# Modulation panels computed in pairs, each 32-column group of TensorE with an output column tile of its own

## The chip, the cores and the metric

One core of a Trainium2 chip (trn2) runs the whole step. The metric is the device time of one execution in microseconds (us); lower is better. Three runs of the kernel before gave 1291.79, 1292.11 and 1295.12 us, median 1292.11.

## The reference, cut to what matters

One layer of a hybrid decoder, for 256 prompt tokens and 8 sequences of 8 sampled tokens (320 tokens, width 1024, all float32). Nine modulation vectors of width 1024 come from the 9 conditioning rows c (one of the prompt, eight of the samples), and shift, scale and gate every branch:

```python
mod = jax.nn.silu(c) @ p['ada_w'] + p['ada_b']          # (9, 1024) @ (1024, 9216)
sh1, sc1, g1, sh2, sc2, g2, sh3, sc3, g3 = jnp.split(mod, 9, axis=-1)
u = rmsnorm(x, norm_ff1) * (1 + sc1) + sh1
x = x + 0.5 * g1 * swiglu(u, ff1_w1, ff1_w3, ff1_w2)    # "up1" (w1, w3) and "down1" (w2)
...                                                     # norm_mix with sh2, sc2; mixer; g2
...                                                     # norm_ff2 with sh3, sc3; "up2", "down2"; g3
```

## The kernel before, in words

**Layout.** Activations stand transposed: features on the 128 partitions, the 320 tokens along the free dimension. Every dense product goes by units of 128 output columns: eight or more blocks of 128 rows of the weights, each an instruction of 128x320 (`mm`, L908). Float32 is split in two parts (`w_hi` + `w_lo`, `u_hi` + `u_lo`), so a unit has three passes of 8 instructions: high by high, low by high, high by low. ScalarE (ACT) makes `w_hi` of a unit two units ahead (`high_ahead`, L1679 to L1690), VectorE (DVE) makes `w_lo` (`low_ahead`, L2304 to L2315).

**The stream.** `unit_order` (L162) writes out the order of all units, and `Stream` gives each a panel in a ring of four 1 MB slots and a PSUM bank. SyncE (SP) loads the panels in that order (`load`, L581); it waits until the unit that last read the slot is done. TensorE (PE) executes its program in order.

**The modulation.** `ada_w` has 36 panels of 1024 x 256 ("ada" units). `ada` (L961) takes the activations as the stationary operand: `c_t` holds silu(c) transposed, 9 columns for each block of 128 rows; the instruction reads 32 columns of it. The array is used as four column groups of 32: block kc goes to group kc % 4 and writes PSUM partitions 32g to 32g+31 with all 256 columns of the panel. So each group holds the sum over two of the eight row blocks, and the four groups must still be added. ACT copies the bank to `mod_row` (`ada_row`, L1692). `mod_columns` (L1046) transposes it by two PE transposes of 128x128 into `aux`. `mod_add` on DVE (L2317) reduces over the four groups (L2321), then adds the bias (L2322).

Panels 0 to 3 hold sh1, 4 to 7 hold sc1, each panel 256 of the 1024 features. These eight are ahead of "up1", in the order `ADA_HEAD` = 4, 0, 5, 1, 6, 2, 7, 3. The other 28 follow later two at a time, behind units of up1 (18 panels, L37), down1 (6, L38) and up2 (4, L39). There the transposes of two panels are issued just ahead of the next two panels (`panel`, L1126).

**The front.** The order of each engine is written out by hand. PE (L1078 to L1103): transposes of c; panel 4; transposes of the packed parameters; then the panels one by one, each followed by `mod_columns` of the one before; x is turned (`turn_x`, three transposes for each of 8 blocks) in two halves, behind the second and the third panel; the sum of squares behind the fourth. ACT (L1782 to L1801): `ada_row` of each panel, squares and copies of x in two halves, the table load for the square root (`load_root`), `root`, `first_norm_high` of the four pairs of feature blocks (L1716), with `w_hi` of up1's first unit ahead of the fourth. DVE (L2416 to L2433):

```python
            for i in range(4):
                mod_add(st.at["ada", ADA_HEAD[i]])
            dve.wait_ge(S["x_read"], KD)
            inverse_root(0)
            mod_add(st.at["ada", ADA_HEAD[4]])
            first_norm(0)
            mod_add(st.at["ada", ADA_HEAD[5]])
            first_norm(1)
            first_norm(2)
            mod_add(st.at["ada", ADA_HEAD[6]])
            first_norm_low(0)
            mod_add(st.at["ada", ADA_HEAD[7]])
            first_norm(3)
            first_norm_low(1)
```

`first_norm(pair)` (L2404) makes the gain (L2409) and two tiles x * gain / rms (L2337). ACT adds the shift (L1714), POOL does the same for the sampled tokens (L706, L707) and ACT copies those (L1675). `first_norm_low` (L2412; L2352, L2345) makes the low parts. Up1's first two units run in one piece (`dense_two`, L910).

Of the kernel before, what the change touches and what calls it, by code (L numbers as in the profile page):

```python
# [7 lines left out]
ALU = mybir.AluOpType  # L8
# [27 lines left out]
ADA_HEAD = (4, 0, 5, 1, 6, 2, 7, 3)  # L36
# [22 lines left out]
def ada_place(p):  # L59

    return ADA_HEAD.index(p) if p < len(ADA_HEAD) else p

# [21 lines left out]
class Stream:  # L84
# [12 lines left out]
    def __init__(self, order):  # L97
# [4 lines left out]
        for name, q in order:  # L102
# [99 lines left out]
def build(nc, io, out):  # L202
# [5 lines left out]
    with ctx:  # L208
# [444 lines left out]
        def _(pool):  # L653
# [41 lines left out]
            def first_samples():  # L695
# [65 lines left out]
            def row_fills():  # L761

                pool.wait_ge(S["gates_mm"], 1)
                pool.wait_ge(S["mod_turned"], ADA_LAST_DOWN + 1)
# [137 lines left out]
        def _(pe):  # L902
# [58 lines left out]
            def ada(u):  # L961
                w = panel_dst(u)
                pe.wait_ge(slot_in[u.slot], u.arrivals)
                if u.uses:
                    pe.wait_ge(bank_free[u.bank], u.uses)
                for kc in range(KD):
                    g = kc % 4
                    ins = mm(banks[u.bank][32 * g:32 * g + 32, 0:256], c_t[:, NSEQ * kc:NSEQ * kc + 32], w[:, kc, :], kc < 4, kc >= 4)
                ins.then_inc(unit_done, 1)

            def shift_rows(n, shift, u):

                pe.wait_ge(slot_in[u.slot], u.arrivals)
                pe.wait_ge(S["mod_read"], 4 * shift + 8)
# [71 lines left out]
            def mod_columns(u):  # L1046
# [38 lines left out]

            for i, a in enumerate(ADA_HEAD):
                u = st.at["ada", a]
                ada(u)
                if a == ADA_HEAD[0]:
# [4 lines left out]
                if i > 0:  # L1094
                    mod_columns(st.at["ada", ADA_HEAD[i - 1]])
                if i == 1 or i == 2:
                    for kc in range(4 * (i - 1), 4 * i):
                        turn_x(kc)
                if i == 3:
# [3 lines left out]
            mod_columns(st.at["ada", ADA_HEAD[-1]])  # L1103
# [22 lines left out]
            def panel(u, pending):  # L1126

                if u.q % 2 == 0:
                    for v in pending:
                        mod_columns(v)  # L1130
                    pending = []
                ada(u)
                return pending + [u]
# [47 lines left out]
            for u in st.of("qk"):  # L1181
# [9 lines left out]
                if u.q == 4:  # L1191
                    pe.wait_ge(S["gate_lin"], 1)
                    pe.wait_ge(S["mod_read"], ADA_LAST_DOWN + 1)
# [477 lines left out]
        def _(act):  # L1671
# [20 lines left out]
            def ada_row(u):  # L1692
                p = ada_place(u.q)
                act.wait_ge(unit_done, u.done)
                if p >= 2:
                    act.wait_ge(S["mod_turned"], p - 1)
                copy(mod_row[p % 2][:, :], banks[u.bank][:, 0:256]).then_inc(bank_free[u.bank], 1)
# [18 lines left out]
            def first_norm_high(pair):  # L1716
                for kc in range(2 * pair, 2 * pair + 2):
# [64 lines left out]
            for i, a in enumerate(ADA_HEAD):  # L1782
                u = st.at["ada", a]
                ada_row(u)
# [3 lines left out]
                if i == 1 or i == 2:  # L1788
                    for kc in range(4 * (i - 1), 4 * i):
                        act.wait_ge(S["x_turned"], kc + 1)  # L1790
                        nc.scalar.activation(sq[:, kc, :], aux[kc % 2][:, 0:T], ACT.Square).then_inc(S["sq_ready"], 1)
                        copy(x_t[:, kc, :], aux[kc % 2][:, 0:T]).then_inc(S["x_read"], 1)
                if i == 2:
                    load_root()
                if i == 3:
                    root(0)
                if i >= 5:
                    first_norm_high(i - 5)
# [491 lines left out]
        def _(dve):  # L2290
# [820 lines left out]
```

## Time and profile before

| what | value |
|---|---|
| time, median of three runs | 1292.11 us |
| span of the profiled execution | 1291.4 us |
| PE busy | 1256.7 us, 97% of the span |
| DVE busy | 782.7 us, 61% |
| ACT busy | 624.3 us, 48% |
| DMA over the span | 241.57 MB, 187 GB/s |

The span is all that the profile gives of the profiled execution's own time; it lies 0.7 us below the median of the three runs. In the profile, PE is TensorE's matmul side and PEld its weight loads. "PEclk" and the last columns of the windows give the clock that TensorE was granted, as a part of full speed. In rows of the timeline the first number is the start, the second the length of the stretch from the first start to the last end, and xN the number of instructions. A float32 matmul or transpose of the `ada` kind is two instructions in the trace for one in the code (a panel is x16 for eight calls); a transpose is one.

### The profile page before, as it was taken

To read this page: it belongs to the slowest core of one execution; us is meant where nothing else is said; L and a number is where in the kernel's file an instruction comes from. 1 tells how busy PE (TensorE), PEld (TensorE's weight loads), DVE (VectorE), ACT (ScalarE), POOL (GpSimd) and SP (SyncE) were. 2 spreads that over 40 slices of the span, in tenths; PEclk is the share of its full clock that TensorE was granted. 3 is DMA by queue.
4 is the path that set the end of the run, shared out by engine and by line. 5 is a ranking of instruction groups with operands and counts; after the bars stand their busy time and mean duration, and the time that the engine had idled before them with its cause. 6 is when DMAs were issued, how large, how long until landed. Compare 5 with 4: busy or idle time off the path is not lost.

```text
span 1291.4 us, 22833 instructions
## 1 busy us (share of the span) xinstructions
PE 1256.7 (97%) x9132; PEld 1152.1 (89%) x9132; DVE 782.7 (61%) x1368; ACT 624.3 (48%) x1101; POOL 222.3 (17%) x393
## 2 busy tenths in 40 slices
PE   6899999999999899999999999999999999999997
PEld 3699999999997777779999889888999989999997
DVE  0734444545896456856379877865576884554433
ACT  3433333434757646655356675554652453333432
POOL 4100000011551222211023333322500310000000
PEclk9899999999999999999999999999999999999998
DMA  9976777776333689886664375464436446554541
GB/s 281 247 242 212 244 252 231 215 221 208 99 99 112 219 281 334 297 278 191 188 196 143 111 212 167 136 205 149 132 108 186 133 129 208 184 164 131 152 141 41
DMA packets 258863, 241.57 MB, mean 187 GB/s; under 512 B 8607, under 2 KB 242479, under 8 KB 258710
## 3 DMA queue, kind: packets, MB, share of 16 engines
q1 hardware_dynamic: 249262, 211.03, 53.7%
q0 software_dynamic: 9024, 28.91, 6.7%
q8 instruction: 73, 1.20, 0.4%
q10 hardware_dynamic: 472, 0.17, 0.1%
q14 instruction: 32, 0.26, 0.1%
HBM read 209.88 MB, written 30.21 MB: 186 GB/s over the span
## 4 chain that ended last, share of the span: by engine, by line
PE 61%; DVE 5%; ACT 2%; issue 1%; POOL 0%; ACTq 0%; DVEq 0%; POOLq 0%
PE bank L908 52%; PE aux L908 6%; PE aux L905 2%; DVE w_lo L2313 1%; DVE arena L2526 1%; PE bank L905 1%; ACT w_hi L1689 1%; DVE arena L2524 0%; ACT arena L1675 0%; DVE stats L2758 0%; ACT vp L1675 0%; DVE arena L2530 0%; ACT u_hi L1714 0%; POOL arena L751 0%; DVE arena L2337 0%
## 5 line engine op out<-in xcount | busy, mean ns | idle before, releaser
L2313 DVE TENSOR_TENSOR w_lo<-ring,w_hi 128x1024 fp32r<-128x1024 f32 (+1 forms) x264 | 336.8, 1276 | 374.9 <-ACT w_hi L1689 370.4
L1689 ACT ACTIVATE w_hi<-ring 128x1024 fp32r<-128x1024 f32 (+1 forms) x264 | 289.7, 1097 | 505.4 <-PE bank L908 486.3
L908 PE MATMUL bank<-u_hi,w_hi 128*128 128x320 f32 x1504 | 264.0, 317 | 4.1 <-issue 1.5
L908 PE MATMUL bank<-u_hi,w_lo 128*128 128x320 f32 x1504 | 251.3, 309 | 0.4 <-DVE w_lo L2313 0.4
L908 PE MATMUL bank<-u_lo,w_hi 128*128 128x320 f32 x1504 | 250.6, 309 | 0.0
L908 PEld LDWEIGHTS bank<-u_hi,w_hi 128*128 128x128 f32 x1504 | 228.8, 189 | 20.9 <-issue 14.0
L908 PEld LDWEIGHTS bank<-u_hi,w_lo 128*128 128x128 f32 x1504 | 228.1, 188 | 0.9 <-DVE w_lo L2313 0.9
L908 PEld LDWEIGHTS bank<-u_lo,w_hi 128*128 128x128 f32 x1504 | 228.2, 188 | 0.0
L905 PE MATMUL aux<-ident,arena 128*128 128x128 f32 (+5 forms) x408 | 61.7, 282 | 14.8 <-ACT arena L1778 8.7
L905 PEld LDWEIGHTS aux<-ident,arena 128*128 128x128 f32 (+5 forms) x408 | 45.5, 145 | 27.3 <-issue 16.5
L713 POOL TENSOR_TENSOR arena<-x_t,gain 128x64 f32<-128x64 f32 x16 | 4.8, 299 | 354.8 <-DVE x_t L2385 354.8
L908 PE MATMUL bank<-ff_hi,w_hi 128*128 128x320 f32 x352 | 57.8, 311 | 0.0
L908 PE MATMUL bank<-ff_hi,w_lo 128*128 128x320 f32 x352 | 56.8, 308 | 0.0
L908 PE MATMUL bank<-ff_lo,w_hi 128*128 128x320 f32 x352 | 56.8, 308 | 0.0
L908 PEld LDWEIGHTS bank<-ff_hi,w_hi 128*128 128x128 f32 x352 | 52.6, 188 | 1.6 <-issue 1.6
L908 PEld LDWEIGHTS bank<-ff_hi,w_lo 128*128 128x128 f32 x352 | 52.9, 187 | 0.0
L908 PEld LDWEIGHTS bank<-ff_lo,w_hi 128*128 128x128 f32 x352 | 52.9, 187 | 0.0
L1675 ACT ACTIVATE arena<-bank 128x256 f32<-128x256 f32 (+4 forms) x134 | 43.3, 355 | 17.5 <-PE bank L908 14.5
L691 POOL TENSOR_TENSOR arena<-arena 128x320 f32<-128x320 f32 x12 | 10.4, 869 | 239.9 <-ACT arena L1701 226.5
L908 PE MATMUL bank<-arena 32*128 32x128 f32 (+6 forms) x496 | 51.0, 355 | 0.4 <-DVE arena L2920 0.4
L2526 DVE SCALAR_TENSOR_TENSOR arena<-arena,par 128x344 f32<-128x344 f32 x80 | 46.7, 583 | 3.9 <-POOL arena L751 1.8
L908 PE MATMUL bank<-y_hi,w_hi 128*128 128x320 f32 x272 | 45.8, 309 | 0.0
(390 smaller groups left out, 1617.2 us busy)
## 6 DMA issues: line engine op xcount, KB each, us to landing
ring<-in_w_in SPq DMA_DIRECT2D x52, 1024.0 KB, 5.6
ring<-in_ff_w SPq DMA_DIRECT2D x44, 1024.0 KB, 5.5
ring<-in_ada_w SPq DMA_DIRECT2D x36, 1024.0 KB, 7.3
ring<-in_ff_w SPq DMA_DIRECT2D x32, 704.0 KB, 4.7
arena<-in_state_mlstm_C SPq DMA_DIRECT2D x22, 512.0 KB, 6.3
out_s_C<-arena POOLq DMA_DIRECT2D x22, 512.0 KB, 5.8
ring<-in_w_pa SPq DMA_DIRECT2D x8, 1024.0 KB, 6.6
arena<-in_state_ssm SPq DMA_DIRECT2D x32, 256.0 KB, 4.6
```

The lines of the kernel that those rows point to most:

```text
L691: ins = nc.gpsimd.tensor_tensor(sq[:, 0, :], sq[:, 0, :], sq[:, kc, :], ALU.add)
L713: nc.gpsimd.tensor_tensor(sequences(xg_s[n][:, kc, :]), sequences(x_t[:, kc, TP:T]), gain[:, kc, 1:NSEQ].unsqueeze(2).to_broadcast([128, S ...
L905: return nc.tensor.transpose(dst, src, ident[0:rows, 0:rows])
L908: return nc.tensor.matmul(dst, lhs, rhs, start=first, stop=last)
L1675: return nc.scalar.activation(dst, src, ACT.Copy, scale=scale)
L1689: nc.scalar.activation(w_hi[v.split_no % 2][:, 0:v.kc, :], panel_part(v), ACT.Copy).then_inc(S["hi_done"], 1)
L2313: V.tensor_tensor(w_lo[r][:, 0:v.kc, :], panel_part(v), w_hi[r][:, 0:v.kc, :].bitcast(FP32), ALU.subtract)\
L2526: ch.link(V.scalar_tensor_tensor(out=a, in0=p[:, tap:tap + CONVW], scalar=par[:, c + w_col + tap * tiles:c + w_col + tap * tiles + 1], in1 ...
```

## The change

- The panels are computed two at a time (`ada_pair`). Column groups 0 and 1 take the two 128-column halves of the first panel, groups 2 and 3 those of the second. Every group runs over all eight row blocks, so nothing is left to be added up over groups. A pair writes 128 columns of one bank instead of 256 columns of two.
- ACT copies 128 columns once for a pair, PE transposes once instead of four times, and DVE does one addition of the bias straight out of PSUM (128 x 36) instead of two reductions and two additions. `mod_read` and `mod_turned` now count pairs.
- `ADA_HEAD` becomes 4, 5, 0, 1, 6, 7, 2, 3: scale of the first half, shift of the first half, scale and shift of the second half.
- The front is rewritten for pairs: x is turned whole behind the first pair; ACT and DVE have new orders; `first_norm_high`, `first_norm_low` and POOL's part now wait for the pair that holds their shift.

```diff
-ADA_HEAD = (4, 0, 5, 1, 6, 2, 7, 3)
+ADA_HEAD = (4, 5, 0, 1, 6, 7, 2, 3)
...
 def ada_place(p):
-    return ADA_HEAD.index(p) if p < len(ADA_HEAD) else p
+    return (ADA_HEAD.index(p) if p < len(ADA_HEAD) else p) // 2
...
+            if second_of_pair(name, q):          # name == "ada" and q % 2 == 1
+                u.opens = False
+                bank_at[name, u.own] = bank_at[name, u.own - 1]
...
@@ POOL, first_samples @@
                     pool.wait_ge(S["xr_ready"], 2 * pair + 1)
+                    pool.wait_ge(S["mod_read"], panels_read(pair) + 1)
...
@@ PE @@
-            def ada(u):
-                w = panel_dst(u)
-                pe.wait_ge(slot_in[u.slot], u.arrivals)
-                if u.uses:
-                    pe.wait_ge(bank_free[u.bank], u.uses)
-                for kc in range(KD):
-                    g = kc % 4
-                    ins = mm(banks[u.bank][32 * g:32 * g + 32, 0:256], c_t[:, NSEQ * kc:NSEQ * kc + 32], w[:, kc, :], kc < 4, kc >= 4)
-                ins.then_inc(unit_done, 1)
+            def ada_pair(first, second):
+                for u in (first, second):
+                    pe.wait_ge(slot_in[u.slot], u.arrivals)
+                if second.uses:
+                    pe.wait_ge(bank_free[second.bank], second.uses)
+                for kc in range(KD):
+                    for g in range(4):
+                        u = (first, second)[g // 2]
+                        ins = mm(banks[u.bank][32 * g:32 * g + 32, 0:128], c_t[:, NSEQ * kc:NSEQ * kc + 32],
+                                 panel_dst(u)[:, kc, g % 2 * 128:(g % 2 + 1) * 128], kc == 0, kc == KD - 1)
+                        if kc == KD - 1 and g % 2:
+                            ins.then_inc(unit_done, 1)
...
@@ mod_columns @@
-                for j in range(2):
-                    ins = turn(aux[2 + r][:, j * 128:(j + 1) * 128], mod_row[r][:, j * 128:(j + 1) * 128], 128)
-                ins.then_inc(S["mod_turned"], 1)
+                turn(aux[2 + r][:, 0:128], mod_row[r][:, 0:128], 128).then_inc(S["mod_turned"], 1)
...
@@ PE, the front @@
+            for i, (first, second) in enumerate(head):
+                ada_pair(first, second)
+                if i == 0:
...                                              (transposes of the parameters, as before)
+                    for kc in range(2):
                         turn_x(kc)
+                    mod_columns(second)
+                    for kc in range(2, KD):
+                        turn_x(kc)
+                if i == 1:
+                    mod_columns(second)
                     pe.wait_ge(S["x_read"], KD)
                     sum_squares_most(0)
                     sum_squares_last(0)
+                if i >= 2:
+                    mod_columns(second)
...
@@ ACT, the front @@
+            for i in range(4):
+                ada_row(st.at["ada", ADA_HEAD[2 * i + 1]])
                 if i == 0:
...                                              (par, as before)
+                    for kc in range(KD):
...                                              (square and copy of x, as before)
+                    load_root()
+                if i == 1:
+                    root(0)
                 if i == 2:
+                    first_norm_high(0)
+                    first_norm_high(1)
+            first_norm_high(2)
             high_ahead(st.at["ada", ADA_HEAD[-1]], st.at["up1", 0])
             first_norm_high(3)
...
@@ DVE, mod_add @@
-                m = mod[:, 2 * p:2 * p + 2, :]
-                ch.link(V.tensor_reduce(m, aux[2 + r][:, 0:256].rearrange("p (j g s) -> p j s g", j=2, g=4)[:, :, 0:NSEQ, :], AX.X, ALU.add))
-                V.tensor_tensor(m, m, par[:, 2 * p:2 * p + 2].unsqueeze(2).to_broadcast([128, 2, NSEQ]), ALU.add).then_inc(S["mod_read"], 1)
+                V.tensor_tensor(mod[:, 2 * p - 2:2 * p + 2, :], aux[2 + r][:, 0:128].rearrange("p (g s) -> p g s", g=4)[:, :, 0:NSEQ],
+                                par[:, 2 * p - 2:2 * p + 2].unsqueeze(2).to_broadcast([128, 4, NSEQ]), ALU.add).then_inc(S["mod_read"], 1)
...
@@ DVE, the front @@
+            mod_add(st.at["ada", 5])
             dve.wait_ge(S["x_read"], KD)
             inverse_root(0)
             first_norm(0)
             first_norm(1)
+            mod_add(st.at["ada", 1])
+            first_norm_low(0)
+            mod_add(st.at["ada", 7])
             first_norm(2)
             first_norm(3)
             first_norm_low(1)
+            mod_add(st.at["ada", 3])
             first_norm_low(2)
             low_ahead(st.at["ada", ADA_HEAD[-1]], st.at["up1", 0])
             first_norm_low(3)
```

## Rows read from the trace of the kernel before

**Rows 1.** The page: busy time, share of the span, instructions.
```profile
PE 1256.7 (97%) x9132; PEld 1152.1 (89%) x9132; DVE 782.7 (61%) x1368; ACT 624.3 (48%) x1101; POOL 222.3 (17%) x393
```

**Rows 2.** Windows: length, busy (x) of PE, PEld, DVE, ACT, POOL, clock, DMA, GB/s.
```profile
53.20:320.00 266.80, 266.79 (x2075) 252.00 (x2076) 131.46 (x225) 98.31 (x141) 9.42 (x16) 1.00 0.75 228
```

**Rows 3.** Timeline, a late pair of panels between two units of up1.
```profile
86.13 0.60 PE L905 MATMUL aux<-ident,arena 128*128 128x128 f32 x4
...
86.66 1.45 PEld L908 LDWEIGHTS bank<-ring,c_t 128*32 128x32 f32 x32 [0.17 <-issue]
86.66 1.93 PE L908 MATMUL bank<-ring,c_t 128*32 128x256 f32 x32
```

**Rows 4.** The tile c_t: all weight loads of the panels, min/median/max ns.
```profile
L908 PEld LDWEIGHTS bank<-ring,c_t x576: 106/110/178, 10.0 to 1122.5; 128*32 128x32 f32 x192
```

**Rows 5.** Timeline, narrow windows (86.9 and 87.05 on) of that pair.
```profile
86.90 0.13 PEld L908 LDWEIGHTS bank<-ring,c_t 128*32 128x32 f32 x4
...
86.66 0.64 PE L908 MATMUL bank<-ring,c_t 128*32 128x256 f32 x8
...
86.66 0.85 PE L908 MATMUL bank<-ring,c_t 128*32 128x256 f32 x12
```

**Rows 6.** Timeline: a copy to w_hi that waited for its DMA, and the unit that uses it.
```profile
165.01 1.06 ACT L1689 ACTIVATE w_hi<-ring 128x1024 fp32r<-128x1024 f32 x1 [3.18 <-DMA ring<-in_ff_w]
...
169.95 1.29 PE L908 MATMUL bank<-u_hi,w_hi 128*128 128x320 f32 x7
```

**Rows 7.** Timeline of the front: PE and what it feeds, to the reciprocal.
```profile
14.84 0.45 ACT L1675 ACTIVATE par<-aux 128x336 f32<-128x336 f32 x1 [2.34 <-PE aux L905]
...
16.43 1.93 PE L908 MATMUL bank<-ring,c_t 128*32 128x256 f32 x16 [1.63 <-DMA ring<-in_ada_w]
...
19.74 0.44 ACT L1791 ACTIVATE arena<-aux 128x320 f32<-128x320 f32 x1 [0.93 <-PE aux L905]
...
20.66 0.44 ACT L1791 ACTIVATE arena<-aux 128x320 f32<-128x320 f32 x1
...
30.70 1.30 PE L908 MATMUL aux<-arena,ones 128*128 128x320 f32 x4
...
31.93 1.07 PE L908 MATMUL bank<-ring,c_t 128*32 128x256 f32 x16
32.03 0.53 ACT L1709 ACTIVATE rs<-aux,eps_col 128x320 f32<-128x320 f32 x1 [1.02 <-PE aux L908]
...
33.77 2.14 DVE L2331 RECIPROCAL rs<-rs 128x320 f32<-128x320 f32 x1
```

**Rows 8.** Timeline of the front, from the gains to up1's first units.
```profile
38.53 0.17 DVE L2409 SCALAR_TENSOR_TENSOR gain<-mod,par 128x18 f32<-128x18 f32 x1
...
38.74 0.95 DVE L2337 SCALAR_TENSOR_TENSOR arena<-x_t,gain,rs 128x256 f32<-128x256 f32 x2
...
39.53 0.90 ACT L1714 ACTIVATE u_hi<-arena,mod 128x256 fp32r<-128x256 f32 x2
...
40.48 0.31 ACT L1675 ACTIVATE u_hi<-arena 128x128 fp32r<-128x128 f32 x1
...
41.39 0.28 DVE L2352 TENSOR_TENSOR u_lo<-arena,u_hi 128x128 fp32r<-128x128 f32 x1
41.60 1.03 DVE L2345 SCALAR_TENSOR_TENSOR u_lo<-arena,mod,u_hi 128x256 fp32r<-128x256 f32 x2
...
42.19 1.04 ACT L1689 ACTIVATE w_hi<-ring 128x1024 fp32r<-128x1024 f32 x1
...
53.21 1.40 PE L908 MATMUL bank<-u_hi,w_hi 128*128 128x320 f32 x8
```

**Rows 9.** Windows of the front (columns as rows 2).
```profile
18.30:24.20 5.90, 5.90 (x34) 2.87 (x30) 0.41 (x2) 3.45 (x9) 2.59 (x3) 1.00 1.09 348
...
43.30:50.00 6.70, 6.58 (x29) 5.85 (x30) 6.50 (x13) 2.16 (x4) 0.99 (x2) 0.66 1.02 203
```

**Rows 10.** DMA issues of the panel asked for at 30.3 us.
```profile
ring<-in_ada_w SPq DMA_DIRECT2D x1, 1024.0 KB, 5.1
```

More of the change, by code:

```diff
@@ L59, in ada_place, with panels_read, second_of_pair @@
 def ada_place(p):
-    return ADA_HEAD.index(p) if p < len(ADA_HEAD) else p
+    return (ADA_HEAD.index(p) if p < len(ADA_HEAD) else p) // 2
+def panels_read(end):
+    return ada_place(end)
+def second_of_pair(name, q):
+    return name == "ada" and q % 2 == 1
 def high_at(norm, kc):
@@ L1084, in _ @@
             pe.wait_ge(S["small_made"], 2)
[L1086 to L1089, printed above, removed]
+            head = [(st.at["ada", ADA_HEAD[i]], st.at["ada", ADA_HEAD[i + 1]]) for i in range(0, len(ADA_HEAD), 2)]
+            for i, (first, second) in enumerate(head):
+                ada_pair(first, second)
+                if i == 0:
                     pe.wait_ge(S["packs_in"], 11 * 16)
@@ L1093, in _ @@
                     turn(aux[0][:, 216:336], pk[0:120, 2, :], 120).then_inc(S["front_turned"], 1)
[L1094 to L1097, printed above, removed]
+                    for kc in range(2):
                         turn_x(kc)
-                if i == 3:
+                    mod_columns(second)
[3 more added lines that the diff above has]
+                    mod_columns(second)
                     pe.wait_ge(S["x_read"], KD)
@@ L1130, in panel @@
                         mod_columns(v)
-                    pending = []
-                ada(u)
-                return pending + [u]
+                    return []
+                ada_pair(st.at["ada", u.q - 1], u)
+                return [u]
             for u in st.range(("up1", 0), ("up1", 2 * KF - 1)):
@@ L1693, in ada_row @@
                 p = ada_place(u.q)
+                if not second_of_pair(u.name, u.q):
+                    return
                 act.wait_ge(unit_done, u.done)
@@ L1696, in ada_row @@
                     act.wait_ge(S["mod_turned"], p - 1)
-                copy(mod_row[p % 2][:, :], banks[u.bank][:, 0:256]).then_inc(bank_free[u.bank], 1)
+                copy(mod_row[p % 2][:, 0:128], banks[u.bank][:, 0:128]).then_inc(bank_free[u.bank], 1)
             def square(n, kc):
@@ L1716, in first_norm_high @@
             def first_norm_high(pair):
+                act.wait_ge(S["mod_read"], panels_read(pair) + 1)
                 for kc in range(2 * pair, 2 * pair + 2):
@@ L1787, in _ @@
                     copy(par[:, :], aux[0][:, 0:336]).then_inc(S["front_read"], 1)
-                if i == 1 or i == 2:
-                    for kc in range(4 * (i - 1), 4 * i):
+                    for kc in range(KD):
                         act.wait_ge(S["x_turned"], kc + 1)
@@ L2406, in first_norm @@
                 k = slice(2 * pair, 2 * pair + 2)
-                dve.wait_ge(S["mod_read"], 2 * pair + 2)
+                dve.wait_ge(S["mod_read"], panels_read(4 + pair) + 1)
                 g = par[:, 72 + 2 * pair:74 + 2 * pair].unsqueeze(2).to_broadcast([128, 2, NSEQ])
@@ L2412, in first_norm_low @@
             def first_norm_low(pair):
+                dve.wait_ge(S["mod_read"], panels_read(pair) + 1)
                 samples_low(0, 2 * pair, 2 * pair + 2)
                 tiles_low(0, 0, 2 * pair, 2 * pair + 2)
-            for i in range(4):
-                mod_add(st.at["ada", ADA_HEAD[i]])
+            mod_add(st.at["ada", 5])
             dve.wait_ge(S["x_read"], KD)
             inverse_root(0)
-            mod_add(st.at["ada", ADA_HEAD[4]])
             first_norm(0)
-            mod_add(st.at["ada", ADA_HEAD[5]])
             first_norm(1)
+            mod_add(st.at["ada", 1])
+            first_norm_low(0)
+            mod_add(st.at["ada", 7])
             first_norm(2)
-            mod_add(st.at["ada", ADA_HEAD[6]])
-            first_norm_low(0)
-            mod_add(st.at["ada", ADA_HEAD[7]])
             first_norm(3)
             first_norm_low(1)
+            mod_add(st.at["ada", 3])
             first_norm_low(2)
@@ L2441, in panel @@
                         mod_add(v)
-                    pending = []
-                return pending + [u]
+                    return []
+                return [u]
             for u in st.range(("up1", 0), ("up1", 2 * KF - 1)):
```

19 lines of the change are left out of this document (5 added, 14 removed).

## The prediction

> **What bounds the kernel now.** I read the page first: PE is busy for 1256.7 of 1291.4 us [rows 1]. Then windows: from the third unit of up1 to the start of the mixer PE is busy for 266.79 of 266.80 us [rows 2]. So behind the front a microsecond of work taken from PE is a microsecond gained, and work taken from ACT or DVE is worth nothing. The front (0 to 53.21 us) is another matter: there PE waits, and the path changes hands. The timeline shows it: PE with the panels and x until 31.9 us, root and reciprocal until 35.91 us [rows 7], then DVE, ACT and POOL by turns make u until ACT copies the first `w_hi` at 42.19 us, and the third unit of up1 starts at 53.21 us [rows 8]. Both places have to be costed, and they have different signs.
>
> **Part 1: the 14 pairs behind the front.** There are 576 matmuls of this kind, 32 for a pair, so 18 pairs [rows 4]; four lie in the front, 14 behind it. Before, a pair is 32 matmuls in eight sets of four that run side by side. The sets are 0.85 - 0.64 = 0.21 us apart [rows 5], and the pair takes 1.93 us with the end of the last one [rows 3]. After, there are 64 matmuls in sixteen sets, each over half the columns: 0.107 us a set if the columns set the pace, so 1.93 us again. The unknown is the weight loads, 64 for a pair in place of 32. Below: the loads of a set lie beside the matmuls of the set before, as now (32 loads keep PEld busy for 1.45 us inside the 1.93 us [rows 3]), and cost nothing; they can't gain anything, since the columns are the same. Above: the four loads of a set take 0.13 us [rows 5], and a set cannot be shorter than that: 16 x 0.13 = 2.08 against 1.71 us, 0.37 us a pair. I take nothing, because the recorded load (110 ns [rows 4]) is longer than a load keeps its successor waiting: these 128x128 transposes also need loads, and four of them with theirs went by in 0.60 us with the last one's end.
>
> PE's transposes fall from four to one for a pair. Four start 0.53 us before the panels' first matmul [rows 3]; that is 0.13 us each with the change to column groups, which stays. Without it I take half the pitch of a 256-column set, 0.11 us: 3 x 0.11 = 0.33 us a pair, 4.6 us for 14 pairs (5.6 us by 0.13).
>
> ACT's one copy for two and DVE's one addition for four instructions are hidden by PE and earn nothing. The first panel's slot comes free only at the end of the pair, 0.9 us later; SP's queue behind it (the next panels) starts later by that. What covers it: where ACT already waits for a DMA, the copy at 165.01 us, done at 166.07, is used at 169.95 [rows 6], 3.9 us of cover; seven copies wait so, and none of them has less than 3 us. If the cover were gone, it would cost up to 0.9 us for each of nine pairs in up1.
>
> Here a rule of the Trainium skill speaks against the change. In the trace, loads ran beside matmuls of all four column groups [rows 3, 5]. The page "TensorE: Matmul & The Clock Gate" (Part 3: Packing small matmuls) says that a load overlaps with matmuls in flight only when the row group differs; here every group uses all rows. By that rule twice the loads would stand open, which is the third rival below; the trace does not agree with it.
>
> **Part 2: the front up to the reciprocal.** The first pair needs the panel that PE waited for until 16.43 us [rows 7]; that stays. At half clock a panel took 1.93 us at 16.43 and 1.07 us at 31.93 [rows 7], which is TensorE's lower level (1.2 GHz) and its upper one (2.4 GHz); PE had then been busy without a break since 16.43. First pair: 3.7 us, to 20.1. Then three transposes of the parameters (some 0.8 us), ACT's copy of them (0.45 us), on which x now waits, and 0.93 us until ACT has the first block of x [rows 7]: 22.3 us. Blocks follow every 0.92 us (19.74, 20.66 [rows 7]), with one transpose between: the last is turned at 29.0 us. Second pair: half clock until about 31, as before, then full: 31.9 us (30.8 if the clock is up from the start, 32.7 if not at all). ACT's copy and one transpose, 0.6; sum of squares 1.30; root 0.53; reciprocal 2.14 [rows 7]: it ends at 36.5 us, against 33.77 + 2.14 = 35.9. Call this end R; 0.6 us later, between 0.5 us earlier and 1.4 later.
>
> **Part 3: the front from R on.** Now the hand-written order of DVE decides. Steps [rows 8]: the gain and two tiles 1.16 us (38.53 to 39.69); two tiles by ACT and the samples' copy behind POOL 1.3 us (39.53 to 40.79); low parts of a pair 1.24 us (41.39 to 42.63); `mod_add` now one instruction, 0.2 us. The sum: two gains with tiles 2.3; `mod_add` of the second pair, which ACT's first high part now needs, 0.2; ACT 1.3; low(0) 1.25; `mod_add` 0.2; two more gains with tiles 2.3; low(1) 1.25; only then `mod_add` of the last pair, which holds the shift of blocks 4 to 7, 0.25; ACT's high(2) 1.3: R + 10.35. ACT has `w_hi` of up1 behind that, 1.04, and PE starts at R + 11.5 = 48.0 us. Before, it started at 43.3, R + 7.4, as the shift was there before and only the tiles were waited for. So 4.7 us later: 4.1 from the order, 0.6 from R. From there to the third unit it was 9.9 us; at mean clock 0.66 in 43.3 to 50 [rows 9], so half clock for 4.6 us. PE had nearly stood still from 37 us on. It stands still for longer now, so I keep the half-clock stretch; but blocks 6 and 7 are less behind: 9.4 us. The front's end is then 4.7 - 0.5 = 4.2 us later. Nothing absorbs it: PE has no idle time afterwards.
>
> Cover in the front: the last two panels are asked for when the second pair is done, 31.9 us, since it holds slots 2 and 3. One asked for with an empty queue landed after 5.1 us [rows 10], the next follows 3.0 us behind (1.05 MB at 348 GB/s [rows 9]): 40.0 us. Half clock 3.7, copy and transpose 0.6: 44.3 us, and DVE asks for it at R + 8.85 = 45.3. Covered by 1.0 us. Up1's first panel lands 3 us behind, at 43, needed at 46.9. POOL's waits for the shifts lie inside the 1.3 us.
>
> **The sum.** +4.2 - 4.6 = -0.4. The profiled span of 1291.4 is 0.7 us below the median; against the median 1292.1 it gives 1291.7 us. About 0.3%, 3.9 us, is what a measurement of this kernel can tell from no change, so this is no change: a gain in the middle given away in the front.
>
> **Rivals.**
> 1. *The front costs almost nothing: faster.* The clock rises during the first pair, a denser stretch than any before, and is still up when up1 starts: R is 1.1 us earlier, the 4.6 us at half clock give back up to 2.3, of which I count 1.8, and the transposes are worth 0.13 each (1.0 more). 1291.7 - 3.9 = 1287.8 us. For it: 3.7 us of panels without a break. Against: PE stands for some 4 us before up1, and it came down before with less. Chance 0.14.
> 2. *The loads set the pace: slower.* In `ada_pair`, the four loads of a set take 0.13 us, the columns 0.107. It decides from the point where a set lasts over 0.13 us: 0.37 us a pair, 5.2 us for 14, which eats the transposes: 1296.9 us. For it: twice the loads with half the work over each. Against: they start together and lie over each other. Chance 0.17.
> 3. *The loads are not hidden at all,* the rule above: 16 x 0.13 = 2.1 us a pair on top, 29 us for 14, 1321 us. Against it stand the rows of before. Chance 0.02.
> 4. *The transposes were not on the path,* because what ends last is ACT's or DVE's copy of the weights: then only the front's 4.2 us stand, 1296.3 us. Against: PE never waited [rows 2]. Chance 0.05.
>
> The forecast has 0.62; its own range is 1289 to 1295.5 us (R from -1.1 to +0.8 about my value, loads up to 0.1 us a pair, transposes 0.11 to 0.13). Faster by over 0.3% is rival 1: 0.14. Slower is rivals 2 to 4: 0.24. Within: 0.62. The range that holds it 8 times in 10 reaches to rivals 1 and 2: 1288.0 to 1297.0.
>
> **What the profile after would show.** Part 1: 64 matmuls of 128x128 in about 1.9 us for a pair, one transpose ahead; over 2.2 us means rival 2. Part 2: reciprocal ends near 36.5. Part 3: first `w_hi` copy near 47 us in place of 42.2, with DVE the engine that ACT waited for; third unit near 57.4. I am wrong if up1 starts before 45 us, if a pair gets shorter than 1.8 us, or if PE waits for a panel in up1.

## The result and the profile after

The change made the kernel a little slower: 1296.49 us (1294.19 to 1297.53, 20 runs) against 1293.34 us (1289.78 to 1296.94, 20 runs) for the kernel before on the same chip. The ratio is 1.0019, interval 1.0012 to 1.0025, so +2.5 us of the kernel before. The forecast was 1291.7 us, 0.4 us below the median shown (1292.11). Set on that median the measured ratio is 1294.6 us: within the 0.3% of "no change" and inside the range of 1289 to 1295.5. But the kernel moved the other way than forecast, and its interval excludes no change. The raw median of 1296.49 us lies above that range and inside the wider one (1288.0 to 1297.0). The profiled execution has a span of 1295.1 us and a time of its own of 1296.83 us, 0.3 us above the median, so its rows can be read as those of a typical run.

The page after: span, busy time, share, instructions.
```profile
span 1295.1 us, 23766 instructions
...
PE 1253.9 (97%) x9654; PEld 1165.7 (90%) x9654; DVE 771.9 (60%) x1314; ACT 616.5 (48%) x1083; POOL 222.2 (17%) x393
```
Against [rows 1], PE is busy for 2.8 us less, and the span is 3.7 us longer. So the time is not in PE's work; it lies where PE waits.

**Behind the front.** Windows after (columns as in [rows 2]), from the third unit on:
```profile
57.10:320.00 262.90, 262.90 (x2421) 256.47 (x2422) 123.71 (x189) 92.96 (x129) 9.22 (x16) 1.00 0.76 232
```
Timeline after, the late pair of [rows 3] (start, length, engine):
```profile
90.03 0.27 PE L919 MATMUL aux<-ident,arena 128*128 128x128 f32 x1
90.23 1.69 PEld L922 LDWEIGHTS bank<-ring,c_t 128*32 128x32 f32 x64 [0.21 <-issue]
90.23 1.96 PE L922 MATMUL bank<-ring,c_t 128*32 128x128 f32 x64
...
92.11 1.44 PE L922 MATMUL bank<-u_hi,w_hi 128*128 128x320 f32 x8
```
The tile c_t after, all its weight loads (min/median/max ns):
```profile
L922 PEld LDWEIGHTS bank<-ring,c_t x1152: 106/110/178, 15.4 to 1127.1; 128*32 128x32 f32 x192
```
PE has no gap again. One transpose stands for four, and 64 matmuls take 1.96 us where 32 took 1.93. The 64 loads keep PEld busy for 1.69 us inside them.

**The front**, timeline after, from the first pair to the third unit of up1 (start, length):
```profile
15.48 3.64 PE L922 MATMUL bank<-ring,c_t 128*32 128x128 f32 x64 [5.73 <-DMA ring<-in_ada_w]
...
20.50 7.59 PE L919 MATMUL aux<-ident,arena 128*128 128x128 f32 x25 [0.63 <-ACT par L1693]
...
28.03 3.46 PE L922 MATMUL bank<-ring,c_t 128*32 128x128 f32 x64
...
33.27 1.96 PE L922 MATMUL bank<-ring,c_t 128*32 128x128 f32 x64
...
34.00 2.15 DVE L2350 RECIPROCAL rs<-rs 128x320 f32<-128x320 f32 x1 [10.91 <-ACT rs L1729]
...
41.12 3.64 PE L922 MATMUL bank<-ring,c_t 128*32 128x128 f32 x64 [5.14 <-DMA ring<-in_ada_w]
...
45.17 0.33 PE L919 MATMUL aux<-ident,arena 128*128 128x128 f32 x1 [0.41 <-ACT arena L1693]
45.54 0.20 DVE L2340 TENSOR_TENSOR mod<-aux,par 128x36 f32<-128x36 f32 x1 [0.29 <-PE aux L919]
...
47.02 1.04 ACT L1707 ACTIVATE w_hi<-ring 128x1024 fp32r<-128x1024 f32 x1
...
48.16 4.12 PE L922 MATMUL bank<-u_hi,w_hi 128*128 128x320 f32 x16 [2.65 <-issue]
...
57.09 1.41 PE L922 MATMUL bank<-u_hi,w_hi 128*128 128x320 f32 x8
```
The reciprocal ends at 36.15 (forecast 36.5), the first `w_hi` copy starts at 47.02 (forecast 47), up1 at 48.16 (48.0), the third unit at 57.09 (57.4) where it was 53.21 [rows 8]. Against that one profile the front is 3.9 us later. That so many rows fall on their forecasts is in part luck, as the repeats will show.

**What the forecast had not looked at:** three windows in the middle, after (columns as in [rows 2]), show half clock (1.2 GHz) for 2.2 to 2.8 of their 4 us:
```profile
326.00:330.00 4.00, 4.00 (x22) 4.00 (x22) 4.00 (x9) 0.47 (x1) 0.00 (x0) 0.73 0.00 0
438.00:442.00 4.00, 4.00 (x16) 1.19 (x9) 1.35 (x2) 0.89 (x3) 0.00 (x0) 0.65 0.00 0
1053.00:1057.00 4.00, 4.00 (x22) 4.00 (x22) 4.00 (x9) 0.46 (x1) 0.00 (x0) 0.73 0.00 0
```
The profile of before has the full clock at the same three places of its program. So the two profiles differ by -4.3 us (fourteen pairs), +3.9 (front) and, as the experiments will show, about +4 (three stretches at half clock): together the 3.7 us between the spans. The question is which of these the runs have, and which only these two profiles.

### The profile page after: what moved, and what is told of

It is laid out like the page before. It is cut to its first block, busy times and chain, and to the rows that moved or that the text cites. A ratio compares the mean times of both kernels' runs of the same rounds, so it can differ in the third digit from the quotient of the medians.

```text
span 1295.1 us, 23766 instructions
## 1 busy us (share of the span) xinstructions
PE 1253.9 (97%) x9654; PEld 1165.7 (90%) x9654; DVE 771.9 (60%) x1314; ACT 616.5 (48%) x1083; POOL 222.2 (17%) x393
## 4 chain that ended last, share of the span: by engine, by line
PE 61%; DVE 5%; ACT 2%; issue 1%; POOL 0%; ACTq 0%; DVEq 0%; POOLq 0%
PE bank L922 52%; PE aux L922 6%; PE aux L919 2%; DVE w_lo L2333 1%; DVE arena L2544 1%; PE bank L919 1%; ACT w_hi L1707 1%; DVE arena L2542 0%; ACT arena L1693 0%; DVE stats L2776 0%; DVE arena L2548 0%; ACT vp L1693 0%; ACT u_hi L1734 0%; POOL arena L765 0%; DVE arena L2356 0%
## 5 line engine op out<-in xcount | busy, mean ns | idle before, releaser
L922 PEld LDWEIGHTS bank<-u_hi,w_hi 128*128 128x128 f32 x1504 | 229.5, 190 | 18.3 <-issue 12.2
L919 PE MATMUL aux<-ident,arena 128*128 128x128 f32 (+4 forms) x354 | 54.2, 280 | 11.6 <-ACT arena L1799 8.8
L919 PEld LDWEIGHTS aux<-ident,arena 128*128 128x128 f32 (+4 forms) x354 | 38.9, 145 | 20.4 <-issue 14.1
L922 PE MATMUL bank<-ring,c_t 128*32 128x128 f32 x1152 | 40.1, 298 | 10.9 <-DMA ring<-in_ada_w 10.9
L922 PEld LDWEIGHTS bank<-ring,c_t 128*32 128x32 f32 x1152 | 34.7, 120 | 14.6 <-issue 14.2
```

The lines of the kernel that those rows point to most:

```text
L919: return nc.tensor.transpose(dst, src, ident[0:rows, 0:rows])
L922: return nc.tensor.matmul(dst, lhs, rhs, start=first, stop=last)
```

## The experiments

In all kernels "third unit" is the first matmul of up1's third unit, the first place with nothing to wait for; what comes behind it hardly differs wherever the middle is at full clock: span less third unit is 1238.1 to 1238.3 us in four profiles with the panels as before, and 1233.9 to 1234.4 us in five with the pairs.

**1. The two kernels again, and one half of the change at a time.** `before_again` is the kernel before, unchanged; `after_again` the changed one. In `rear_only` only panels 8 and later go by pairs:
```diff
+def second_of_pair(name, q):
+    return name == "ada" and q >= 8 and q % 2 == 1
...
-                ada(u)
-                return pending + [u]
+                    return []
+                ada_pair(st.at["ada", u.q - 1], u)
+                return [u]
```
`front_only` is the reverse: the eight panels of the front by pairs with the new front order, panels 8 and later as before.

> The kernel before once more, for a second profile. Theory A: its span may this time hold one or more stretches at half clock at the stalls near 322, 434 and 1046 us, each worth 1.1 to 1.7 us, and the profile of before was merely free of them. Theory B: none in the middle again. Ratio 1.000 in both.

> The changed kernel once more, for a second profile. Theory A (granted clock by luck): the stretches at half clock near 325, 437 and 1052 us of the first profile come from where the chip's grid of clock decisions happens to lie against three stalls that both kernels have; then this profile shows other ones, or none, the time stays about 2.4 to 3 us over the kernel before. Theory B (they belong to the change): the same three stretches again, at the same stalls.

> Pairs only for the 28 panels behind the front; the eight of the front and the whole front as before. By the sum of the prediction (transposes 0.33 us a pair, loads hidden): 4.4 us faster than before, ratio 0.9966. If weight loads or something else behind the front ate the gain: ratio 1.000 or above. If the half-clock stretches belong to the pairs behind the front: about 4 us of the gain is missing and the profile shows them.

> Pairs only for the eight panels of the front, with the new order of x, ACT and DVE; the 28 panels behind as before. By the sum of the prediction: third unit of up1 starts 3.9 to 4.2 us later and nothing gives it back: ratio 1.0032. If the front's loss is absorbed later: 1.000. If it also moves stalls so that half clock is granted more often: over 1.004.

| kernel | median us (lowest to highest, runs) | ratio to before, interval |
|---|---|---|
| before_again | 1294.74 (1291.06 to 1297.35, 12) | 1.0014, 1.0001 to 1.0027 |
| after_again | 1295.25 (1293.64 to 1297.71, 12) | 1.0020, 1.0007 to 1.0032 |
| rear_only | 1288.41 (1286.17 to 1293.73, 12) | 0.9973, 0.9958 to 0.9988 |
| front_only | 1300.27 (1299.78 to 1301.45, 6) | 1.0059, 1.0042 to 1.0076 |

The two halves have opposite signs, as forecast: the pairs behind the front gain, the front loses. `front_only` lost more than expected: 0.0059, where the sum gave 0.0032 and the interval starts at 0.0042. Its profile shows one part of it: behind the third unit it takes 1241.8 us instead of 1238.2, 3.6 us more, and two stretches at half clock near 438 and 1054 us make up about 3.1 of them. The two halves together (-3.5 and +7.6 us) give 4.1 us where the whole change gave 2.5; their intervals of about 2 us each leave open whether they simply add. The repeat of the unchanged kernel shows how little one ratio can carry here: 1.0014 with nothing changed. And its profile has a front of another length, in the same instructions. Timeline of `before_again`:
```profile
15.92 1.93 PE L908 MATMUL bank<-ring,c_t 128*32 128x256 f32 x16 [1.70 <-DMA ring<-in_ada_w]
21.88 1.93 PE L908 MATMUL bank<-ring,c_t 128*32 128x256 f32 x16
27.25 1.07 PE L908 MATMUL bank<-ring,c_t 128*32 128x256 f32 x16
...
31.74 2.15 DVE L2331 RECIPROCAL rs<-rs 128x320 f32<-128x320 f32 x1
...
40.17 1.04 ACT L1689 ACTIVATE w_hi<-ring 128x1024 fp32r<-128x1024 f32 x1
...
51.17 1.40 PE L908 MATMUL bank<-u_hi,w_hi 128*128 128x320 f32 x8
```
The fourth panel already goes at the full clock (1.07 us at 27.25); in the profile shown, PE was at half clock until about 31 us. The third unit is 2.0 us earlier. In `rear_only` the third panel was already fast, and the third unit stood at 50.61:
```profile
21.64 1.07 PE L921 MATMUL bank<-ring,c_t 128*32 128x256 f32 x16
```
The changed kernel's front varies as much. `after_again` has the same three stretches at half clock in the middle, but its third unit is 3.3 us earlier than in `after`:
```profile
19.14 2.77 PE L919 MATMUL aux<-ident,arena 128*128 128x128 f32 x13 [0.63 <-ACT par L1693]
...
30.86 2.15 DVE L2350 RECIPROCAL rs<-rs 128x320 f32<-128x320 f32 x1 [9.97 <-ACT rs L1729]
...
53.84 1.40 PE L922 MATMUL bank<-u_hi,w_hi 128*128 128x320 f32 x8
```
A warning on one column: for 18.3 to 24.2 us [rows 9] prints a clock of 1.00, though the panel in that stretch took 1.93 us, the time at half clock. In the front the panels' lengths are the better guide. Timeline of the kernel before:
```profile
22.39 1.93 PE L908 MATMUL bank<-ring,c_t 128*32 128x256 f32 x16
```

**2. The clock behind the front taken away.** The fill is work that changes no output: matmuls of 128 columns into columns of a bank that nobody reads, where PE waits behind the first gate of a branch and ahead of the state's tails.
```diff
+            def warm(dst, n):
+                for _ in range(n):
+                    mm(dst[:, 384:512], ident[:, :], ones[:, :])
...
                     for kc in range(KD):
+                        if i == 0:
+                            warm(aux[3], (2, 0, 1, 1, 3, 1, 1, 1)[kc])
                         pe.wait_ge(S["u_hi_ready"], high_at(n, kc))
...
+                if n == 1:
+                    pe.wait_ge(S["n_new"], 1)
+                    pe.wait_ge(S["den_read"], 1)
+                    warm(banks[2], 12)
```
(The eight numbers add up to 10 for each branch; the expectation of `after_warm` says 11.) The fill went into the kernel before, into `rear_only` and into the changed one. The fourth kernel, `front2`, is the changed one with another front order and no fill: the second pair stands between the two halves of x, both halves' sums are done ahead of the third pair, third and fourth pair go one behind the other with their transposes behind both, and DVE adds the columns of a pair as soon as they are there:
```diff
             mod_add(st.at["ada", 5])
+            mod_add(st.at["ada", 1])
             dve.wait_ge(S["x_read"], KD)
             inverse_root(0)
             first_norm(0)
             first_norm(1)
-            mod_add(st.at["ada", 1])
-            first_norm_low(0)
             mod_add(st.at["ada", 7])
+            mod_add(st.at["ada", 3])
             first_norm(2)
+            first_norm_low(0)
             first_norm(3)
             first_norm_low(1)
-            mod_add(st.at["ada", 3])
             first_norm_low(2)
```

> The same filling in the kernel before, which showed no half clock behind these stalls in two profiles. Theory clock: nothing to gain or at most 1 us (some of its runs have a lower mean clock), ratio 0.999 to 1.000. If filling shortens the kernel by 3 us here too, it is not what sets the two kernels apart.

> Pairs only behind the front, with the filling. Theory clock: the one stretch of half clock (429 us) is gone, and the whole 4.4 us of the transposes shows: ratio 0.9955 to 0.9965, against 0.9973 without the filling.

> The changed kernel with idle TensorE work (matmuls of constants into unused PSUM columns) put into the three stalls behind which half clock was granted: 11 ahead of up1's successors' normed units each time, 12 ahead of the second tails' transpose. Theory clock (the pairs move the stalls to where the clock falls, and that is the missing 3 to 4 us): no half clock at 321, 434 and 1048 us any more, 3.5 to 4 us faster than the changed kernel, ratio to before 0.999. Theory other (the half clock is an accident of the profiled runs and the loss lies elsewhere): ratio stays at 1.002 or rises with the extra work.

> The changed kernel with another order in the front alone: second pair between the two halves of x (so that its slots are free 5 us earlier), third and fourth pair next to each other, and DVE adds both ahead of the third gain. By the prediction's part 3, the order cost 4.1 us from the reciprocal on; this should give most of it back: up1 starts near 43.5 us in place of 48 (45 in the second profile), 4 us faster than the changed kernel, ratio near 0.999. If the front's loss came from the clock alone, no change: 1.002.

| kernel | median us (lowest to highest, runs) | ratio to before, interval |
|---|---|---|
| before_warm | 1290.60 (1288.46 to 1291.47, 9) | 0.9979, 0.9969 to 0.9989 |
| rear_warm | 1285.90 (1284.82 to 1288.25, 5) | 0.9946, 0.9934 to 0.9959 |
| after_warm | 1292.49 (1290.73 to 1293.47, 11) | 0.9996, 0.9984 to 1.0008 |
| front2 | 1294.03 (1292.15 to 1294.46, 11) | 1.0006, 0.9996 to 1.0017 |

Windows of `after_warm` at the same three places:
```profile
326.00:330.00 4.00, 4.00 (x30) 4.00 (x29) 4.00 (x10) 1.06 (x2) 0.00 (x0) 1.00 0.00 0
438.00:442.00 4.00, 4.00 (x27) 2.98 (x22) 2.99 (x3) 1.16 (x3) 0.77 (x1) 1.00 0.01 4
1053.00:1057.00 4.00, 4.00 (x30) 4.00 (x29) 3.93 (x10) 2.53 (x3) 0.00 (x0) 1.00 0.28 82
```
The first window holds 30 matmul instructions where the changed kernel had 22. Each stretch cost 1.16 to 1.64 us by the shift of what follows it. What PE did ahead of the first, in the changed kernel's timeline:
```profile
322.68 1.12 PE L922 MATMUL bank<-u_hi,w_hi 128*128 128x320 f32 x4 [0.60 <-ACT u_hi L1693]
...
324.38 1.84 PE L922 MATMUL bank<-u_hi,w_hi 128*128 128x320 f32 x4 [0.59 <-ACT u_hi L1734]
...
326.02 2.29 PE L922 MATMUL bank<-u_hi,w_lo 128*128 128x320 f32 x8
```
Two waits of 0.6 us for ACT, then a pass of eight matmuls in 2.29 us where it takes 1.33. The profile of before has the same two waits (0.58 and 0.59 us) and no half clock behind them, so the wait alone does not decide it. (Ahead of the second stretch stands one wait of 2.8 us, in both kernels.) All three stretches are in both profiles of the changed kernel and in that of `front2`, two in `front_only`, one in `rear_only`, none in two of before.

But my expectation that before gains at most 1 us by the fill fell: it gained 2.3 to 2.7 us, so many of its runs have such stretches too. The mean clocks of the timed runs bear this out. Of the 67 runs of before beside these kernels, 26 have 0.994, as the profile of `before_again`, with a median of 1291.30 us; the other 41 have 0.989 to 0.992, with a median of 1293.93. With the middle filled, all nine have 0.993 or 0.994. So both profiles of before are of the quicker kind, and `before_again`'s (1291.06 us) was the fastest of its twelve runs.

By the ratios the fill gains 3.0 us for the changed kernel and 2.7 us for before. The stretches explain what the two profiles differ by behind the front; of what the medians differ by they explain 0.3 us, give or take some 2 us by their intervals.

With the fill behind the front, the changed kernel is still 1.9 us slower than before (2.2 by the ratios), and 6.6 us slower than the pairs alone. That is most of the measured change, and it is in the front. `rear_warm` gained more than the 0.9955 to 0.9965 that I expected, since before itself gains by the fill.

`front2` shows which part of the front is the order of DVE and ACT. Its timeline:
```profile
34.05 2.15 DVE L2355 RECIPROCAL rs<-rs 128x320 f32<-128x320 f32 x1 [4.42 <-ACT rs L1734]
36.16 1.96 PE L922 MATMUL bank<-ring,c_t 128*32 128x128 f32 x64 [0.90 <-DMA ring<-in_ada_w]
...
42.09 1.04 ACT L1712 ACTIVATE w_hi<-ring 128x1024 fp32r<-128x1024 f32 x1
...
52.80 1.40 PE L922 MATMUL bank<-u_hi,w_hi 128*128 128x320 f32 x8
```
The first `w_hi` copy starts 5.9 us behind the reciprocal's end, where the changed kernel took 10.9 and the one before 6.3 (42.19 - 35.91). From the reciprocal's end to the third unit it takes 16.6 us, where before took 17.3 and the changed kernel 20.9: the order alone takes back all that Part 3 of the prediction counted as lost. But the reciprocal itself ends at 36.20, late as in the changed kernel. The third unit at 52.80 is 4.3 us earlier than in `after` and 1.0 us earlier than in `after_again`. The ratio with its unfilled middle is 1.0006, 1.7 us better than the changed kernel and not the 4 that I expected.

**3. The half clock in the front taken away too.** More fill of the same kind (`ident` by `ident`), in the waits of the front: in `before_hot` and `rear_hot` 6 ahead of the first panel, 6 around the parameters' transposes, 10 and 3 ahead of the last two panels' transposes, 5 behind them; in `after_hot`
```diff
+                if i == 0:
+                    hot(10, 3)
+                if i == 3:
+                    hot(20)
                 ada_pair(first, second)
...
                 if i >= 2:
                     mod_columns(second)
+                if i == 3:
+                    hot(18)
```
and in `front2_hot` 10, 6 and 14 at the same places.

> The kernel before with the fill of before_warm and, in the front too, 30 more matmuls of 128 columns whose result nobody reads, where TensorE waits for DMA or for ScalarE. My theory (the chip gives the front's first full clock at 19 to 31 us from one run to the next, and half clock once more behind the front's last waits; both are only luck of how busy TensorE was): the clock rises by 20 us in the profile, the 6.8 us at half clock near 37 to 41 us are gone or shorter, the reciprocal ends at 32 to 33 us, the third unit starts near 48.5 instead of 49.5, and the time is 1288.5 to 1290.5, 0.5 to 2 us under before_warm's 1290.6. Rival (the front is bound by DMA and by VectorE, its clock costs nothing): 1290.6, no change.

> Pairs only behind the front, with the fill of rear_warm and the same 30 matmuls in the front as in before_hot. Fourteen pairs are worth 0.31 us each plus the first-unit shifts, 4.3 to 4.7 us: so before_hot less 4.5, 1284.0 to 1286.0. Rival as for before_hot: 1285.9, as rear_warm.

> The change with the fill of after_warm and 48 such matmuls in the front: 10 ahead of the first pair, 20 ahead of the fourth pair while it waits for its DMA, 18 behind its transpose. My theory (the new front loses 4.5 us from the reciprocal on by VectorE's order and has nothing to do there with the clock; what it loses ahead of the reciprocal is mostly the clock): reciprocal end near 34, dense start near 46, third unit near 55, time 1289.5 to 1291.5, some 5 us over rear_hot and 0 to 1.5 over before_hot. Rival (the front's loss is the clock, which the filled front does not have): within 2 us of rear_hot, under 1288.

> The other front order (both halves of x around the second pair, column adds ahead of the reciprocal) with the fill behind the front and 30 such matmuls in the front. My theory: front2's reciprocal was late (36.2) for its clock and for the one long row of work ahead of it, and its order from there on costs only 7 us to the first copy of weights as before, so with a warm clock the third unit starts near 50.5 and the time is 1285 to 1287.5, near rear_hot. Rival (with eight panels by pairs in the front the reciprocal stays at 36 whatever the clock, since it waits for ScalarE's sixteen passes over x): 1289.5 to 1291.

| kernel | median us (lowest to highest, runs) | ratio to before, interval |
|---|---|---|
| before_hot | 1290.64 (1288.90 to 1292.16, 8) | 0.9976, 0.9964 to 0.9989 |
| rear_hot | 1285.81 (1285.10 to 1287.50, 5) | 0.9940, 0.9927 to 0.9952 |
| after_hot | 1289.22 (1287.71 to 1291.14, 6) | 0.9966, 0.9953 to 0.9980 |
| front2_hot | 1286.61 (1285.08 to 1289.33, 6) | 0.9946, 0.9932 to 0.9960 |

Timeline of `after_hot`:
```profile
15.69 1.96 PE L927 MATMUL bank<-ring,c_t 128*32 128x128 f32 x64 [1.41 <-DMA ring<-in_ada_w]
...
24.61 3.33 PE L927 MATMUL bank<-ring,c_t 128*32 128x128 f32 x64
...
30.46 2.15 DVE L2372 RECIPROCAL rs<-rs 128x320 f32<-128x320 f32 x1 [9.98 <-ACT rs L1751]
...
37.65 1.96 PE L927 MATMUL bank<-ring,c_t 128*32 128x128 f32 x64 [0.76 <-DMA ring<-in_ada_w]
...
43.11 1.04 ACT L1729 ACTIVATE w_hi<-ring 128x1024 fp32r<-128x1024 f32 x1
...
44.25 1.51 PE L927 MATMUL bank<-u_hi,w_hi 128*128 128x320 f32 x8
...
52.43 1.40 PE L927 MATMUL bank<-u_hi,w_hi 128*128 128x320 f32 x8
```
First and last pair now take 1.96 us instead of 3.64, and up1 starts at 44.25 instead of 48.16 (48.79 in `after_warm`, but 44.90 in `after_again`, which has no fill). The third unit is at 52.43, earlier than my 55. The second pair, right behind the row of x transposes, still took 3.33 us. It did so in all five profiles with that order: 3.46, 3.35, 3.37 and 2.97 us in `after`, `after_again`, `after_warm` and `front_only`. In `after` and `after_warm` the clock had not come up before it, and the 25 transposes took 7.6 us; in `after_again` and here it had, the transposes took 5.9 and 6.0 us, and the pair behind them was slow all the same.

The fill is worth 3.3 us to the changed kernel (1292.49 to 1289.22) and nothing to the two with the old front (1290.60 and 1290.64; 1285.90 and 1285.81). For these it was a poor control: it is 30 matmuls and not 48, and ten of them stood ahead of a transpose that DVE wanted. The timeline of `before_hot`, where the wait for that transpose is 3.48 us:
```profile
39.38 0.23 DVE L2348 TENSOR_REDUCE mod<-aux 128x18 f32<-128x72 f32 x1 [3.48 <-PE aux L910]
```
There the reciprocal ended at 30.7 us, the earliest of all, and up1 began at 41.10, 3.9 us behind the `w_hi` copy instead of 1.1. So my third unit "near 48.5" was missed (50.67), and how short the old front gets at full clock stays open.

What a filled front says for the change: `after_hot` lies 3.4 us above `rear_hot` (spans 1286.4 against 1283.4, third unit 52.43 against 49.35: 3.0 us). I had expected 5. It also lies 1.4 us below `before_hot`, but the intervals overlap (0.9953 to 0.9980 and 0.9964 to 0.9989), so this is not shown.

`front2_hot`, with the change's panels and the other order, comes to 0.8 us of `rear_hot`, inside both intervals; in the two profiles its third unit is 2.2 us later (51.59 against 49.35). Its timeline:
```profile
22.50 3.64 PE L927 MATMUL bank<-ring,c_t 128*32 128x128 f32 x64
...
33.47 2.15 DVE L2376 RECIPROCAL rs<-rs 128x320 f32<-128x320 f32 x1 [5.18 <-ACT rs L1755]
...
51.59 1.41 PE L927 MATMUL bank<-u_hi,w_hi 128*128 128x320 f32 x8
```
The time is the one that I expected, but for the reciprocal the rival was right: it ends at 35.62 us with the fill, 3.0 us later than in `after_hot`. The second pair stands between the two halves of x and still took 3.64 us, and ACT's last pass over x ended at 30.09 us instead of 25.48. What this order wins, it wins behind the reciprocal: 16.0 us from there to the third unit, against 19.8 in `after_hot`. So that part of the front's loss is the order of the work and not the pairs as such; whether eight panels by pairs can come for nothing is not shown, since the intervals leave some 2 us open.

The fastest versions are `rear_hot` (0.9940), `rear_warm` (0.9946) and `front2_hot` (0.9946), which can't be told apart.

## Why the prediction was wrong

**Part 1, right.** Each of the fourteen pairs moves the program by -0.31 us (forecast -0.33), 4.3 us in all. With equal fills, before less pairs is 4.7 and 4.8 us by the medians and 3.8 and 4.1 by the spans behind the third unit. The pieces add up to more than the spans show, because not quite all is kept: behind the twelfth pair 0.6 to 0.8 us go to longer waits (one, near 566 us, grew from 0.67 to 0.95 us), so "a microsecond taken from PE is a microsecond gained" was a little too strong. The loads are hidden, as taken: a pair is 1.96 us. The cover of the slot that comes free later held, if less than the 3 us that I wrote. Timeline after, the copy of [rows 6]:
```profile
168.51 1.06 ACT L1707 ACTIVATE w_hi<-ring 128x1024 fp32r<-128x1024 f32 x1 [4.03 <-DMA ring<-in_ff_w]
...
172.29 1.44 PE L922 MATMUL bank<-u_hi,w_hi 128*128 128x320 f32 x8
```
It is done at 169.57 and used at 172.29, 2.7 us later.

**Rivals 2, 3 and 4, refuted.** A pair took 1.96 us, against 2.3 for loads that set the pace (rival 2) and some 4 for loads that stand open (rival 3); and `rear_only` gained, so the transposes were on the path (rival 4). The Trainium skill's rule on loads that overlap only across row groups ("TensorE: Matmul & The Clock Gate", Part 3: Packing small matmuls) does not hold for these rows: all four column groups use all rows, and 1.69 us of loads lie inside 1.96 us of matmuls.

**Part 3, the mechanism right and its size too.** From the reciprocal's end to the third unit, the old front took 17.2 to 17.3 us in four profiles (`rear_only`, with 10.2 us at half clock there, took 18.4), the changed one 20.7 to 21.0 in four: +3.6, and the text had 4.1 - 0.5 = 3.6. Its parts were both a little off: up1's start behind the reciprocal +4.5 instead of +4.1, and -0.9 instead of -0.5 from there to the third unit. The last pair's cover of 1.0 us was gone: its DMA ended at 41.12 instead of 40.0, DVE waited 0.29 us for it, and that is its price.

**Part 2 is the step that failed.** It gave +0.6 us up to the reciprocal, from "half clock until about 31, as before" for the second pair. The forecast for the changed kernel is right for the first profile (36.5, measured 36.15), but what it was set against is not what before does: 35.91 us comes from the only one of five profiles with the old front in which the half clock lasted that long. The other four have 33.89, 32.23, 32.35 and 32.59. With all: 33.4 before and, in four profiles with the new front (36.15, 33.01, 35.32, 36.71), 35.3 after, so +1.9 instead of +0.6, and the third unit is 5.3 us later on the mean of the profiles (50.9 to 56.2), not 4.2. Each set spreads over some 3.7 us, so the difference of two means of a few profiles is good to about 2 us. Where the clock came late in both, the reciprocal is only 0.2 to 0.8 us later, as the sum had it.

The timed runs can be asked as well. If the filled middle is at full clock in every run, what lies behind the third unit is as long as in the profile, and a run's span less that is its third unit. This estimate gives 50.6 us (48.4 to 51.4) for the nine runs of `before_warm` and 56.7 us (54.9 to 57.6) for the eleven of `after_warm`: about 6.2 us, with no overlap. Less the 3.6 us of Part 3, Part 2 was worth some 2.6 us and not 0.6.

Why the new front's reciprocal comes later is not shown. The slow second pair behind 25 transposes suggests itself, since the old front puts a panel between the halves of x, and that panel took 1.07 us wherever the clock had come up early. But in `front2` and `front2_hot` a pair stands there too, and took 3.00 and 3.64 us.

**And what the sum left out:** it held PE's clock behind the front as given. With -4.3 and +6.2 the change is at +1.9 us, which agrees with the filled kernels (1.9 to 2.2), as it must, since +6.2 is taken from them; measured without the fill are +2.5 by the ratio. The stretches in the middle, which the changed kernel has in both of its profiles and before only in part of its runs, are left with 0.3 to 0.6 us, less than the intervals can tell from nothing; that the change causes them was not shown, as nothing near those three places was changed.

**Rival 1** (the clock up from the first pair to up1, 1287.8 us) did not happen by itself, but it names the lever: with work put in by hand so that the clock is up for the first and the last pair, the changed kernel comes to 1289.22 us, 3.3 us faster than with the filled middle alone.

## What to carry to other kernels

A gain that is a number of equal pieces on a saturated engine can be forecast to a few hundredths of a microsecond a piece; a front in which engines wait for each other cannot be read off one profile. The old order's was up to 3.7 us longer in one profile than in another, so a change to it should be priced against several executions, with the clock's stretches marked in each. Order each engine's list so that what another engine waits for is not queued behind what could have been done later: the additions queued behind other work cost 3.6 us here, and another order took them back.

## What the runs showed of the hardware that was not expected

- **When TensorE first gets its full clock varies with the same instructions.** With the old front it came at 19 to 31 us, and the third unit stood at 49.53 to 53.21. The latest clock went with the latest third unit.
- **The clock fell behind a row of transposes, without a long wait.** In `after_hot`, PE was at the full clock at 15.7 us (a pair in 1.96 us), had then mostly transposes for 7 us, with waits of at most 0.63 us, and the next pair took 3.33 us. With fourteen transposes ahead of a panel (`rear_only`, 25.59 us) the panel took 1.07 us, its time at full clock; with thirteen between two pairs (`front2_hot`) the second took 3.64.
- **Short waits can be followed by half clock, or not.** Two waits of 0.6 us near 322 us were followed by 3.4 us at half clock in the profiles of the changed kernel and not in the two of before. Such a stretch costs 1.2 to 1.6 us. With small matmuls in the waits it was gone in every profile, and the kernel before was 0.21% faster (0.9979, 0.9969 to 0.9989) with the rest of its work unchanged.
- **Four column groups of 32 take half the columns in half the time.** 64 matmuls of 128 columns took 1.96 us, 32 of 256 columns 1.93 us, with twice the loads.
